# Sparse attention in one layer on one core: where softmax's division is done

## The reference, cut

```python
def dsa_mix(...):                      # blocks of 128 queries, 8 heads
    ...                                # score of every key, the 256 best of each query
    logits = jnp.einsum('bqhc,bqkc->bqhk', ql, kv) * HEAD_DIM ** -0.5
    logits = jnp.where(valid[:, :, None, :], logits, -jnp.inf)
    prob = jax.nn.softmax(logits, axis=-1)
    o_lat = jnp.einsum('bqhk,bqkc->bqhc', prob, kv)          # 128 latent values
    return jnp.einsum('bqhc,chd->bqhd', o_lat, w_uv)         # up to 64 a head
```

## Time and profile before

| | |
|---|---|
| median of three runs | 1809.34 us (1803.66 to 1810.68) |
| the profiled execution | 1810.67 us, of which the span of instructions is 1808.9 us |
| PE busy | 1542.9 us (85%) |
| DVE busy | 915.2 us (51%) |
| ACT busy | 577.7 us (32%) |
| POOL busy | 452.3 us (25%) |
| mean granted TensorE clock | 0.939 of full speed |

### The profile page before, as it was taken

The page is one execution under the profiler, slowest core; times in us unless marked ns, Lnnn a source line. Parts: engine busy times, 40 slices in busy tenths (PEclk is TensorE's granted clock), DMA queues, the critical chain, the costliest instruction groups (busy, mean ns, idle before and its releaser), DMA issues. The chain is left out here.

```text
span 1808.9 us, 45211 instructions
## 1 busy us (share of the span) xinstructions
PE 1542.9 (85%) x17680; PEld 951.3 (53%) x17681; DVE 915.2 (51%) x2100; ACT 577.7 (32%) x1272; POOL 452.3 (25%) x973
## 2 busy tenths in 40 slices
PE   4899999995778788878878699759899999999976
PEld 3644444434666666666666245535455555555542
DVE  3357576455587777686774232533322333333326
ACT  3213897733344344344433011101111111111122
POOL 6401457721011011011000000013333333343320
PEclk8899999996889999999999799779999999999998
DMA  9613534132012110110000365549999999998946
GB/s 326 187 44 124 212 131 172 42 125 79 2 40 83 40 28 13 31 36 13 8 19 7 123 249 174 225 141 406 406 407 407 386 376 370 407 406 337 408 150 255
DMA packets 131916, 334.55 MB, mean 185 GB/s; under 512 B 14372, under 2 KB 52524, under 8 KB 130768
## 3 DMA queue, kind: packets, MB, share of 16 engines
q1 hardware_dynamic: 122528, 313.99, 46.2%
q0 software_dynamic: 9264, 18.86, 3.1%
HBM read 301.00 MB, written 37.25 MB: 187 GB/s over the span
## 5 line engine op out<-in xcount | busy, mean ns | idle before, releaser
L2075 PE MATMUL psX<-arena 128*32 128x256 f32 x5376 | 331.9, 388 | 33.0 <-issue 20.9
L2075 PEld LDWEIGHTS psX<-arena 128*32 128x32 f32 x5376 | 165.9, 111 | 159.1 <-issue 67.8
L2086 PE MATMUL psP<-arena 128*32 128x256 f32 x2688 | 160.4, 379 | 0.5 <-DVE arena L1997 0.5
L811 PE MATMUL psP<-arena 128*128 128x512 f32 x320 | 142.8, 601 | 2.9 <-DVE arena L717 2.9
L511 ACT ACTIVATE arena<-arena 128x1024 bf16<-128x1024 f32 (+5 forms) x138 | 134.3, 973 | 32.5 <-POOL arena L469 28.6
L811 PE MATMUL psX<-arena 128*128 128x512 f32 x320 | 142.6, 600 | 1.9 <-DVE arena L717 1.9
L1985 DVE TENSOR_TENSOR arena<-arena,pair_cols 128x256 f32<-128x256 f32 x85 | 36.2, 426 | 201.3 <-PE psX L2075 201.2
L1759 PE MATMUL psP<-arena 128*128 128x512 f32 x256 | 116.4, 613 | 10.0 <-PEq L114 4.6
L2086 PEld LDWEIGHTS psP<-arena 128*32 128x32 f32 x2688 | 87.2, 110 | 58.2 <-issue 0.6
L1946 ACT ACTIVATE arena<-psX 64x256 f32<-64x256 f32 x84 | 31.7, 377 | 253.0 <-PE psX L2075 253.0
L1904 POOL DMA_INDIRECT arena<-xn_rows,arena x86 | 90.3, 1050 | 75.9 <-POOL arena L1901 71.5
(11 more groups left out here) (407 smaller groups left out, 2619.0 us busy)
## 6 DMA issues: line engine op xcount, KB each, us to landing
arena<-in_e_gate_dram SPq DMA_DIRECT2D x32, 2048.0 KB, 13.2
arena<-in_e_up_dram SPq DMA_DIRECT2D x32, 2048.0 KB, 17.8
arena<-in_e_down_dram SPq DMA_DIRECT2D x32, 2048.0 KB, 15.2
arena<-in_ada_w_dram SPq DMA_DIRECT2D x12, 2048.0 KB, 14.0
proj_T<-arena SPq DMA_DIRECT2D x36, 256.0 KB, 2.0
arena<-in_x_dram SPq DMA_DIRECT2D x16, 512.0 KB, 6.0
arena<-in_w_in_dram SPq DMA_DIRECT2D x4, 2048.0 KB, 8.9
arena<-in_final_ada_w_dram SPq DMA_DIRECT2D x4, 2048.0 KB, 10.3
```

Source lines behind the costliest of these rows:

```text
L811: mm = pe.matmul(psum[b], w[:, k, first:first + P], hT[:, k, 512 * half:512 * half + 512], start=(k == 0), stop=(k == KD - 1))
L2075: mm = pe.matmul(psum["X0"][BLK * c_:BLK * c_ + BLK, 0:DE // 2], xT[:, r, g, :], w[:, 2 * g + r, DE // 2 * h:DE // 2 * (h + 1)], start=(j ...
L2086: mm = pe.matmul(psum["P0"][BLK * g:BLK * g + BLK, 0:QD], hidT[:, f, h, :], down_w[u][:, KE // 2 * h + f, QD * g:QD * g + QD], start=(i == ...
```

## The change

VectorE no longer scales the probabilities head by head. The exponentials go unscaled through the transposes, the value products and the up-projection, and the division is done once per tile on the 128 x 512 result. For that the row sums of the eight heads lie side by side (128 x 8); VectorE takes their reciprocal in one instruction (`row_scale`, at the place of the ninth `next(turns)`); TensorE transposes it to 8 x 128 in bank P1 ahead of the last value product, and ScalarE copies it to a new SBUF tile (`scale_rows`). Behind the up-projection eight small products with a column of the identity, repeated 64 times, as weights spread each head's reciprocals over that head's 64 rows of bank P1. ScalarE's copy of the up-projected rows (now `uv_rows`) stays, and VectorE then multiplies it by the spread reciprocals in place (`mix_dsa`), in one more `next(turns)` at the end of each tile, in the last tile before `centre`.

The negation goes too: the latent queries are scaled by -1/8, the mask is positive, VectorE takes the minimum, and the exponential has scale -1 with that minimum as its bias. TensorE's transposes wait for the exponentials instead of the scaled probabilities.

```diff
-NEG = -1.0e30
+HIDE = 1.0e30
...
+        scale_t = sb("scale_rows", [P, P])
...
+            scale_rows = scale_t[0:NH, :]
...
-            s_mx, s_gn, s_kk = st[:, 40:48], st[:, 48:72], st[:, 72:88]
+            s_least, s_gn, s_kk = st[:, 40:42], st[:, 48:72], st[:, 72:88]
+            s_total, s_scale = (st[:, 0:NH], st[:, NH:2 * NH]), st[:, 2 * NH:3 * NH]
...
-                        link(act, act.activation(qlT[:, 4 * g:4 * g + 4, :], g4(psum[f"X{g}"]), ACT.Copy, scale=HEAD ** -0.5), "qlat", j, g)
+                        link(act, act.activation(qlT[:, 4 * g:4 * g + 4, :], g4(psum[f"X{g}"]), ACT.Copy, scale=-HEAD ** -0.5), "qlat", j, g)
...
-                            act.wait_ge(*at("logits", j, h))
-                            link(act, act.activation(lg[:, h % 2, 0:n], lg[:, h % 2, 0:n], ACT.Exp, bias=s_mx[:, 2 * (h % 2) + 1:2 * (h % 2) + 2],
-                                                     accum_out=s_mx[:, 4 + h % 2:5 + h % 2]), "exps", j, h)
+                            act.wait_ge(*at("lg_masked", j, h))
+                            if h == 0 and j >= 2:
+                                act.wait_ge(*at("row_scale", j - 2))
+                            link(act, act.activation(lg[:, h % 2, 0:n], lg[:, h % 2, 0:n], ACT.Exp, scale=-1.0, bias=s_least[:, h % 2:h % 2 + 1],
+                                                     accum_out=s_total[j % 2][:, h:h + 1]), "exps", j, h)
+                        if h == NH + 1:
+                            act.wait_ge(*at("scale_turned", j))
+                            if j:
+                                act.wait_ge(*at("scale_spread", j - 1))
+                            link(act, act.activation(scale_rows, psum["P1"][0:NH, 0:P], ACT.Copy), "scale_rows", j)
...
-                    link(act, act.activation(mixT[:, 4:8, :], g4(psum["T1"]), ACT.Copy), "mix_dsa", j)
+                    link(act, act.activation(mixT[:, 4:8, :], g4(psum["T1"]), ACT.Copy), "uv_rows", j)
...
-                            link(dve, dve.tensor_tensor_reduce(lg[:, h % 2, 0:n], psum["P"][:, 0:n], mask, 1.0, MASKED, ALU.add, ALU.max, mx), "lg_masked", j, h)
-                            link(dve, dve.tensor_scalar(nmx, mx, -1.0, None, ALU.mult), "logits", j, h)
-                        if h:
-                            b = (h - 1) % 2
-                            sm, rs = s_mx[:, 4 + b:5 + b], s_mx[:, 6 + b:7 + b]
-                            dve.wait_ge(*at("exps", j, h - 1))
-                            step(dve.reciprocal(rs, sm))
-                            link(dve, dve.tensor_scalar(lg[:, b, 0:n], lg[:, b, 0:n], rs, None, ALU.mult), "probs", j, h - 1)
+                            link(dve, dve.tensor_tensor_reduce(lg[:, h % 2, 0:n], psum["P"][:, 0:n], mask, 1.0, BEYOND, ALU.add, ALU.min, s_least[:, h % 2:h % 2 + 1]), "lg_masked", j, h)
+                        else:
+                            dve.wait_ge(*at("exps", j, NH - 1))
+                            if j:
+                                dve.wait_ge(*at("scale_turned", j - 1))
+                            link(dve, dve.reciprocal(s_scale, s_total[j % 2]), "row_scale", j)
                         yield
+                    dve.wait_ge(*at("uv_rows", j))
+                    dve.wait_ge(*at("scale_spread", j))
+                    link(dve, dve.tensor_tensor(mixT[:, 4:8, :], mixT[:, 4:8, :], g4(psum["P1"]), ALU.mult), "mix_dsa", j)
...
+                    next(turns, None)
                 centre(NT - 1)
...
+                        if h == NH + 1:
+                            pe.wait_ge(*at("row_scale", j))
+                            fill(pe, "P1", "scale_rows", j)
+                            pe.transpose(psum["P1"][0:NH, 0:P], s_scale, ident[:, :]).then_inc(*sig("scale_turned", j))
...
-                            pe.wait_ge(*at("probs", j, h - 1))
+                            pe.wait_ge(*at("exps", j, h - 1))
...
-                    fill(pe, "T1", "mix_dsa", j)
+                    fill(pe, "T1", "uv_rows", j)
...
+                    pe.wait_ge(*at("scale_rows", j))
+                    fill(pe, "P1", "mix_dsa", j)
+                    for h in range(NH):
+                        mm = pe.matmul(g4(psum["P1"])[part(h % 2), h // 2, :], ident[0:NH, h:h + 1].to_broadcast([NH, HEAD]), scale_rows, start=True, stop=True)
+                    mm.then_inc(*sig("scale_spread", j))
```

More of the change, by code:

```diff
@@ L445, in _ @@
                 step(pool.memset(scan_reset[:, :].rearrange("p (a b) -> p a b", b=CHUNK)[:, :, 0:1], 0.0))
-                step(pool.memset(causal[0:64, 192:256], NEG))
+                step(pool.memset(causal[0:64, 192:256], HIDE))
                 step(pool.iota(token_id[:, :], pattern=[[P, NT]], base=0, channel_multiplier=1))
@@ L706, in select @@
                     step(dve.tensor_tensor(work[:, 0:n], work[:, 0:n], mask, ALU.add))
-                    step(dve.tensor_scalar(mask, work[:, 0:n], 0.0, NEG, ALU.is_equal, ALU.mult))
+                    step(dve.tensor_scalar(mask, work[:, 0:n], 0.0, HIDE, ALU.is_equal, ALU.mult))
                     yield
@@ L1100, in attention @@
                         if h < NH:
-                            mx, nmx = s_mx[:, 2 * (h % 2):2 * (h % 2) + 1], s_mx[:, 2 * (h % 2) + 1:2 * (h % 2) + 2]
                             if h >= 2:
```

## The result

| | before | after |
|---|---|---|
| median | 1807.04 us (4 runs) | 1776.80 us (4 runs, 1774.64 to 1781.93) |
| ratio, 95% interval | | 0.9838 [0.9812, 0.9864] |
| profiled execution | 1810.67 us | 1776.77 us |

What follows compares the result with a forecast made beforehand. The mix stage was taken as a relay between PE and DVE, neither full. Gain 26.3 us less costs 4.9 (1.2 + 1.8 + 1.9) left 21.4: 1810.7 to 1789.3, or 1788 against the median; range 1774 to 1801.

Steps and rivals of the forecast that it cites:

- What bounds the stage: Mix stage: a relay between PE and DVE; 33.8 us of PE idle ended by DVE directly behind the removed instructions.
- The price of the removed lines and their places: Three DVE instructions per head, with gaps 0.72 us in tile 0 to 1.19 in tile 7; total gain 26.3.
- second levels: Level 2 of tile 6: ScalarE's queue late, its copy moves by 1.25 us, the transposes behind it by 1.56, not 1.93.
- level 5: Tile 6: PE runs on into the next tile's products without a stop, DVE's lead is lost, gain stays at 4.71 us.
- The entry of tile 6: Heads 0 and 1 of tile 6: transposes of head 0 start after 0.90 us idle behind the scaled probabilities; gain 0.90.
- The walk through tiles 2, 3 and 4: Gains followed place by place through each tile's rows up to L1450: 2.15, 2.53 and 3.59 us.
- (a): Added PE transpose of the eight reciprocals before the last value product: 0.15 us a tile, 1.2 in all.
- (c): Eight spreading products behind the up-projection: 1.09 us less 0.84 of PE idle, 0.25 a tile, 1.8 over seven tiles.
- The last tile's 1.9: End of tile 7: spread 1.09, hand-over 0.13, product 0.72 us, uncovered; the tail 1.9 us later, from 1.3 to 2.9.
- I count on the same pattern: PE clock in the mix stage stays as before: mean 0.89 in tiles 0 to 3, 0.97 in 4 to 6, 0.94 after.
- rival 1: Less PE idle in the levels keeps the clock up, 8 us more on the path: 1780 us; chance 0.17.
- Rivals 2 and 4: 2: relay swallows more, gain 13.3, costs 11, about 1806, chance 0.13. 4: PE never waited for them, 1814, chance 0.02.

Runs made afterwards that it cites:

- the second trace: The changed kernel run once more without further change, for another trace and more times: 1780.39 us, ratio 0.9859.
- the second set: The changed kernel with the eight spreading products issued twice, the second time over the first: 1789.0 us, ratio 0.9897.

## Why the prediction was right, and where its sizes were off

- What bounds the stage: right. The idle that VectorE ended directly behind the removed lines went from 33.8 us to 4.4.
- The price of the removed lines and their places: right. 1.18 us a level in tile 7 against 1.19, and second levels (ScalarE's copy late ahead of L1434, 2.1 us in five waits) and level 5 as told. Tiles 5 to 7 at full clock: 16.4 us against 16.2. The entry of tile 6 was mis-sized, 0.90 where full clock gives 1.44, because its row stood behind a low stretch; the next place came out right all the same, at 1.94 against 1.93, so in that step some luck went in.
- The walk through tiles 2, 3 and 4: short. Tiles 2 and 4 gave 7.56 at full clock, not 5.74, and four levels of tile 3 alone 3.15, not 2.53. It went over places at the lower clock, where slow products hide the idle that VectorE ends: in tile 4 none in the row before, 0.99 at full clock. In tile 2 this would be 0.62 of the 1.0, and the rest stays open. For tiles 0 and 1 no pair at full clock was had. Of tile 0's 3.66 at least 1.2 are chance, for in the second trace of the same kernel it gained 2.45.
- The costs: 2.4, not 4.9. The terms that were mis-sized are (a) and (c): the transpose and the spread together show 0.6 us in seven tiles, not 1.05 + 1.8. The transpose shows next to nothing: in tile 7 the up-projection ends 22.86 us behind the start of L1450 before and 22.87 after. The last tile's 1.9 was right: 1.86.
- "I count on the same pattern" of the clock: wrong. The first stretch rose from 0.89 to 0.94, tile 5 fell from full clock. In the mean of the runs this is worth some 2 to 3 us; rival 1 was right in kind, with 8 us it was too large. Its 1780 lies nearer to the measured time than my 1788, but most of the way there is not the clock's.
- Together, at equal clock: 26.3 to 27.2 measured, 21.4 forecast. Of the 4.9 to 5.8 between them 2.5 are the costs, 1.8 the walk in tiles 2 and 4, at least 0.6 tile 3 and 0.2 tiles 5 to 7. What is left, under 1 us, falls to tiles 0 and 1 or lies within the spread of the runs.
- Rival 3 (a spreading product dear because its weights are one column repeated): out, 0.068 us each, as L1310's, and 0.054 each in the second set. Rivals 2 and 4 are out by the waits and by the tiles at full clock.
- The drain at a change of tiling mode, which the Trainium skill states (TensorEngine Tiling (Array Packing), Key Properties): the new rows L1325, L1330 and L1387, three shapes, follow each other every 1.02 us with no idle in front. If there is such a drain, it doesn't show as time here.

## What to carry to other kernels

Follow the relay between two engines tile by tile at the full clock, and treat each level's gain as lost where the other engine runs on without a stop; at full clock that gave tile 7 to 0.01 us and tile 6 to 0.05 at every place but its entry. A row read at the lower clock hides idle that full clock shows, so such places are better read from a trace at full clock. Before trusting one profiled execution, set its mean clock beside that of the other runs: here it was among the lowest, and 0.001 of clock went with 1 us. New work is cheapest in an idle whose end it does not move, and a wait that new work brings (VectorE's for the spread) is itself a place for old work.

## What the runs showed of the hardware that was not expected

Products that nobody reads, put into PE's waits, made the kernels 7.5 us (before) and 8 to 11 us (after, against its two medians) faster: PE's busy time in the stage rose by 14 us and its clock from 0.93 to 0.97 and from 0.95 to 0.98. The Trainium skill (TensorE: Matmul & The Clock Gate, Why this matters for your kernels) advises to avoid idle gaps between bursts of products; the traces agree, and show that the filler need not be useful work.
